# Modulation weights in column blocks: the opening of a hybrid decoder trunk on one core

## The chip, the cores and the metric

The kernel runs on one core of one Trainium2 chip. The metric is device time in microseconds (us). Inputs are float32.

## The reference, cut to what matters

One layer: a conditioning vector c gives shift and scale; the normed tokens are scaled and shifted; one wide projection feeds all branches. The part that the change touches is this.

```
mod = silu(c) @ w_ada + b_ada              # 1024 -> 3072
shift, mscale, gate = split(mod, 3)
h = rms_norm(x, norm_gain) * (1 + mscale) + shift     # (1024 tokens, 1024 features)
proj = h @ w_in                            # q, kv, gates, z_attn, u, z_ssm, merge gates
u = 256 columns of proj                    # input of the state-space branch
...                                        # attention, state space model, merge, final norm
```

Every feature of h needs its own shift and scale, and each of these is a sum over all 1024 entries of silu(c). A block of 128 features of h can be finished as soon as the 2 x 128 columns of w_ada that give its shift and scale are there. The products of u are sums over the 1024 features of h, so they can be accumulated block by block.

## The kernel before, in words

Five engines run queues of their own, in program order, tied by semaphores. What follows is the opening, up to the end of the products of u.

SyncE (SP) issues the large loads: eight tiles of x (L490), four row blocks of w_ada (L488; 128 rows by 2048 columns, 8 KB a row, 1 MB a block), the 256 columns of w_in that give u (L494, 1 MB), four more row blocks of w_ada, and then masks and tables. The next weights (`wraw`, L494) are loaded once the first have been split. GpSimd (POOL) issues 22 small loads for the state-space branch (L609 to L618) and then works through a chain of tiny operations (L601 to L650) that needs two Exp/Sin results of ScalarE.

ScalarE (ACT) takes Exp and Silu of small columns, then squares the eight x tiles as they come (`junk`), with a Sqrt after four and after eight. VectorE (DVE) scales the tiles to unit norm, four at a time (`xs`, L1158). TensorE (PE) transposes them in 16 groups of four (`xt`), evacuated in turn by ACT and DVE (L1163). Then PE sums the modulation: for each of eight row blocks, four matmuls with 32 columns of Silu(c) against 512 columns of w_ada (`ada_mm`), accumulated over all eight blocks into one bank. ACT copies the bank (`mrow`), PE transposes it, and DVE forms `modc` and `g1` for all features at once.

After that DVE, ACT and DVE work block by block (k = 0 to 7, 128 features each): xt times g1 plus modc (L1192), `ht_hi` as its rounded copy, `ht_lo` as the remainder (L1142). PE runs twelve matmuls for each k (four banks, three each: hi by hi, lo by hi, hi by lo) and accumulates u. On DVE the remainder of block k-1 stands behind the scaling of block k. Next on PE come the products of z_ssm (weights `whi[1]`, `wlo[1]`), then those of q. GpSimd waits for the last `ht_lo` and then prepares the state-space kernels, on which PE, ACT and SP rely later.

Of the kernel before, what the change touches and what calls it, by code (L numbers as in the profile page):

```python
# [22 lines left out]
P = 128  # L23
SEQ = 1024
D_MODEL = 1024
KT = D_MODEL // P
# [32 lines left out]
CW = 280  # L59
# [144 lines left out]
def build(nc, x, c, w_ada, b_ada, norm_gain, w_in, pe_cmp_k, w_cmp_k1, b_cmp_k1, w_cmp_k2,  # L204
# [6 lines left out]
    def at(name, shape, dt, offset):  # L211
        return nc.alloc_sbuf_tensor_at(name, shape, dt, offset=offset)
# [4 lines left out]

    ada = at("ada", [P, KT, 2048], F, R_H)
    ht_hi = at("ht_hi", [P, KT, SEQ], R, R_H)
# [28 lines left out]

    mrow = at("mrow", [P, HALF], F, R_W + KT * CW * 4 * 2)
    junk = at("junk", [P, D_MODEL], F, R_W + KT * CW * 4 * 4)  # L250
# [28 lines left out]
    scol = const("scol", [P, KT, 32], F)  # L279
    modc = const("modc", [P, 2 * KT], F)  # L280
    g1 = const("g1", [P, KT], F)
    ss = const("ss", [P, ST], F)
# [199 lines left out]
    with nc.Block() as block:  # L482
# [3 lines left out]
        def _(sp):  # L486
            def load_ada(k):
                sp.dma_start(ada[:, k, :], w_ada[0, P * k:P * k + P, 0:2048]).then_inc(s_blk[k], 16)  # L488
            def load_x(i):
# [107 lines left out]
        def _(pool):  # L597
# [213 lines left out]
        def _(act):  # L811
# [13 lines left out]

            act.wait_ge(once("pcol"), 1)
            a(dt_[:, :], pcol[:, 32:40], ACT.Exp).then_inc(once("dt"), 1)
            a(scol[:, :, :], pcol[:, 48:56].unsqueeze(2).to_broadcast([P, KT, 32]), ACT.Silu).then_inc(s_silu, 1)
            for i in range(ST):
                act.wait_ge(s_x[i], 16)  # L830
                if i >= 1:
                    act.wait_ge(s_sq, i)
                a(junk[:, :], xs[:, i, :], ACT.Square, accum_out=ss[:, i:i + 1]).then_inc(s_sq, 1)
                if i % 4 == 3:
                    act.wait_ge(s_var, i // 4 + 1)
                    a(rs[:, i - 3:i + 1], ss[:, i - 3:i + 1], ACT.Sqrt).then_inc(s_sd, 1)
            for cc in range(NC_HALF):
# [4 lines left out]
            act.wait_ge(once("pw_arg"), 1)  # L842

            a(pw[:, 1, :, :], pw[:, 1, :, :], ACT.Exp).then_inc(once("pw_fn"), 1)
            a(pw[:, 2, :, :], pw[:, 0, :, :], ACT.Sin, scale=SIN_2PI / 2).then_inc(once("pw_fn"), 1)
            a(pw[:, 3, :, :], pw[:, 0, :, :], ACT.Sin, scale=SIN_2PI).then_inc(once("pw_fn"), 1)

            def split_w(w):
# [5 lines left out]

            split_w(0)

            act.wait_ge(s_mod, 1)
            a(mrow[:, :], bank[0]).then_inc(once("mrow"), 1)


            for r in range(2):
                act.wait_ge(once("ctr"), 1)
                a(ct[r][:, :, :], bank[4][:, P * r:P * r + P].rearrange("p (t c) -> p t c", t=SSM_T))\
                    .then_inc(once("ctev"), 1)

            def fill(n):
                act.wait_ge(s_tr, n + 1)
                return bank[n % 2]

            for k in range(KT):  # L870
                for m, cols in enumerate(h_parts(k)):
                    act.wait_ge(s_h32, m + 1 if k == 0 else k + 2)
                    a(ht_hi[:, k, cols], xt[:, k, cols]).then_inc(s_hhi, 1)
            split_w(1)

# [241 lines left out]
            for k in range(KT):  # L1117
                act.wait_ge(s_blk[k], 32)
# [18 lines left out]
        def _(dve):  # L1137
# [26 lines left out]
            dve.wait_ge(s_id, 16)  # L1164
            V.tensor_copy(identb[:, :], ident[:, :]).then_inc(once("identb"), 1)
            dve.wait_ge(once("den"), 1)
            V.reciprocal(sm[:, 9, :], sm[:, 8, :]).then_inc(once("rden"), 1)
            dve.wait_ge(s_whi, 1)
            tt(wlo[0][:, :, 0:256], wraw[:, :, 0:256], f(whi[0][:, :, 0:256]), ALU.subtract).then_inc(s_wlo, 1)
            dve.wait_ge(once("pcol"), 1)  # L1170
            dve.wait_ge(once("mcol"), 1)
            mcol = bank[5].rearrange("p (q r) -> p r q", q=4)[:, ::32, :]
            ch.link(tt(modc[:, :].rearrange("p (b q) -> p b q", b=4), mcol,
                       bcol.rearrange("p (b q) -> p b q", b=4), ALU.add))
            ch.link(V.scalar_tensor_tensor(out=g1[:, :], in0=modc[:, KT:2 * KT], scalar=1.0, in1=gcol,
                                           op0=ALU.add, op1=ALU.mult))
            dve.wait_ge(once("xta"), 8)
# [18 lines left out]
            h_lo(KT - 1)  # L1196
            split_w(1)
            dve.wait_ge(s_small, 16 * 5)
# [385 lines left out]
        def _(pe):  # L1584
# [18 lines left out]

            def ada_mm(k):
                pe.wait_ge(s_blk[k], 16)
                for j in range(4):
                    ins = mm(bank[0][32 * j:32 * j + 32, :], scol[:, k, :], ada[:, k, j * HALF:(j + 1) * HALF],
                             k == 0, k == KT - 1)
                return ins
            pe.wait_ge(s_id, 16)  # L1610
# [3 lines left out]
            for n in range(16):  # L1614
# [10 lines left out]
                ins.then_inc(s_xtr, 1)  # L1625
            pe.wait_ge(s_silu, 1)
            for k in range(KT):
                ins = ada_mm(k)
            ins.then_inc(s_mod, 1)
            pe.wait_ge(once("cld"), 16 * 2 * SSM_T)  # L1630
            pe.wait_ge(once("xta"), 7)
            for r in range(2):
                ins = tr(bank[4][:, P * r:P * r + P], cld[r][:, :])
            ins.then_inc(once("ctr"), 1)
            pe.wait_ge(once("xtd"), 8)
            pe.wait_ge(once("mrow"), 1)
            for q in range(4):
                ins = tr(bank[5][:, P * q:P * q + P], mrow[:, P * q:P * q + P])
            ins.then_inc(once("mcol"), 1)


            def bank_free(n):
# [12 lines left out]


            pe.wait_ge(s_whi, 1)
            pe.wait_ge(s_wlo, 1)
            for k in range(KT):
                pe.wait_ge(s_hlo, 1 if k == 0 else k + 2)  # L1660
                for i in (0, 2, 1, 3):
                    ct_, cc = divmod(i, 2)
                    if k == 0 and i == 1:
                        pe.wait_ge(s_hlo, 2)
# [4 lines left out]
            ins.then_inc(s_unit, UU)  # L1669

            def project(w, tiles=range(ST)):
# [433 lines left out]
```

## Time and profile before

| | us |
|---|---|
| median of 3 runs | 992.6 (991.83 to 993.16) |
| the profiled execution, its own time | 991.09 |
| span in its trace | 989.3 |
| TensorE busy in the span | 910.2 (92%) |
| VectorE busy | 528.5 (53%) |
| ScalarE busy | 394.5 (40%) |
| GpSimd busy | 215.7 (22%) |

The span runs from the first to the last instruction; 1.8 us of the execution lie around it. TensorE's busy time overstates its work, since matmuls overlap. In the 40 slices of the profile TensorE is at nine tenths or more in nearly all slices; the two first slices (0 to 49 us) are the exception, with none and seven tenths, while the DMA engines are at nine tenths there.

### The profile page before, as it was taken

How to read it: one execution, taken by the hardware profiler on the slowest of the kernel's cores; microseconds unless marked ns; L12 is line 12 of the kernel's file. 1: busy time of each engine (PE TensorE's matmuls, PEld its weight loads, DVE VectorE, ACT ScalarE, POOL GpSimd, SP SyncE). 2: the span in 40 equal slices, each digit the busy share in tenths (PEclk: the TensorE clock that was granted, in tenths of full speed). 3: DMA queues.
4: the chain of work that ended last, by engine and by line, in shares of the span. 5: the costliest groups of instructions: out<-in, count | busy, mean ns of one | idle time of the engine just before them, and what ended most of it. 6: DMA issues, size and time to landing. Idle time of an engine off the chain costs nothing.

```text
span 989.3 us, 14340 instructions
## 1 busy us (share of the span) xinstructions
PE 910.2 (92%) x5573; PEld 745.6 (75%) x5581; DVE 528.5 (53%) x1075; ACT 394.5 (40%) x786; POOL 215.7 (22%) x213
## 2 busy tenths in 40 slices
PE   0799999899999999999998998889999999999996
PEld 0488999689999766666676766678888888877885
DVE  1561279426765487797786876552231222217543
ACT  5533232422123466767657667641111111114121
POOL 6249512111100112212203212145551000000000
PEclk9999999899999999999999999989999999999998
DMA  9917041031010000000000001043322112033222
GB/s 314 356 44 128 4 111 65 1 88 45 1 44 1 2 1 1 1 1 1 2 1 1 1 2 32 7 123 96 100 71 70 53 33 59 16 154 127 87 85 85
DMA packets 53716, 59.67 MB, mean 60 GB/s; under 512 B 10097, under 2 KB 45489, under 8 KB 52609
## 3 DMA queue, kind: packets, MB, share of 16 engines
q1 hardware_dynamic: 51392, 54.13, 18.3%
q0 software_dynamic: 2000, 4.54, 1.6%
q8 instruction: 44, 0.72, 0.3%
q14 instruction: 24, 0.19, 0.1%
q10 hardware_dynamic: 256, 0.09, 0.0%
HBM read 52.92 MB, written 5.24 MB: 59 GB/s over the span
## 4 chain that ended last, share of the span: by engine, by line
PE 71%; DVE 14%; ACT 6%; SPq 3%; issue 3%; DMA 2%; POOL 0%; DVEq 0%; ACTq 0%; POOLq 0%
PE bank L1588 39%; PE slc_max L1588 15%; PE win_max L1588 13%; PE bank L1591 3%; DVE plo L1142 3%; SPq L488 2%; DVE rt L1142 2%; DVE mx L1410 2%; DMA ada<-in_w_ada 2%; ACT pt L815 1%; DVE mx L1417 1%; ACT phi L815 1%; ACT osb L815 1%; DVE qa L1142 1%; SPq L527 1%
## 5 line engine op out<-in xcount | busy, mean ns | idle before, releaser
L1142 DVE TENSOR_TENSOR plo<-pt,phi 128x512 fp32r<-128x512 f32 x192 | 116.2, 621 | 36.8 <-ACT phi L815 36.4
L815 ACT ACTIVATE pt<-bank 128x512 f32<-128x512 f32 (+1 forms) x208 | 98.7, 474 | 83.3 <-PE bank L1588 77.2
L1588 PE MATMUL bank<-q,k 128*128 128x512 f32 (+7 forms) x384 | 102.7, 349 | 0.9
L815 ACT ACTIVATE phi<-bank 128x512 fp32r<-128x512 f32 (+1 forms) x208 | 98.5, 474 | 0.0
L601 POOL TENSOR_TENSOR qa<-qa,otmp 128x256 f32<-128x256 f32 x32 | 27.5, 859 | 215.2 <-DVE otmp L1142 215.2
L1588 PEld LDWEIGHTS bank<-q,k 128*128 128x128 f32 (+1 forms) x384 | 63.4, 190 | 11.9 <-ACT phi L815 2.9
L1588 PE MATMUL bank<-phi,vhi 128*65 128x512 f32 x192 | 70.1, 365 | 2.4 <-ACT osb L815 1.9
L1588 PE MATMUL bank<-phi,vlo 128*64 128x512 f32 x192 | 62.0, 323 | 0.0
L1588 PE MATMUL bank<-plo,vhi 128*65 128x512 f32 x192 | 61.9, 323 | 0.0
L1588 PE MATMUL bank<-ht_hi,dhi 128*128 128x512 f32 x128 | 50.6, 396 | 2.8 <-DVE at_lo L1142 2.8
L1410 DVE TENSOR_REDUCE mx<-slc_max 128x1 f32<-128x128 f32 (+3 forms) x64 | 48.1, 752 | 8.7 <-PE slc_max L1588 8.7
L815 ACT ACTIVATE dsig<-bank 128x512 f32<-128x512 f32 x16 | 9.6, 599 | 105.3 <-PE bank L1588 105.3
L1588 PE MATMUL win_max<-whi,ht_hi 128*128 128x256 f32 (+1 forms) x160 | 47.5, 297 | 4.2 <-ACT catc L815 4.2
L1588 PE MATMUL bank<-ht_lo,dhi 128*128 128x512 f32 x128 | 50.3, 393 | 0.0
L1588 PE MATMUL bank<-ht_hi,dlo 128*128 128x512 f32 x128 | 50.3, 393 | 0.0
L1588 PE MATMUL bank<-whi,ht_hi 128*128 128x256 f32 (+1 forms) x160 | 46.6, 291 | 0.0
L1588 PE MATMUL win_max<-wlo,ht_hi 128*128 128x256 f32 (+1 forms) x160 | 46.4, 290 | 0.0
L1588 PE MATMUL win_max<-whi,ht_lo 128*128 128x256 f32 (+1 forms) x160 | 46.3, 289 | 0.0
L1588 PE MATMUL bank<-wlo,ht_hi 128*128 128x256 f32 (+1 forms) x160 | 45.3, 283 | 0.0
L1588 PE MATMUL bank<-whi,ht_lo 128*128 128x256 f32 (+1 forms) x160 | 45.2, 283 | 0.0
L1417 DVE TENSOR_REDUCE mx<-win_max 128x1 f32<-128x640 f32 (+2 forms) x64 | 41.4, 648 | 0.0
L1142 DVE TENSOR_TENSOR mt<-bank,dsig 128x512 f32<-128x512 f32 x8 | 5.5, 692 | 63.3 <-ACT dsig L815 54.3
(395 smaller groups left out, 2535.8 us busy)
## 6 DMA issues: line engine op xcount, KB each, us to landing
ada<-in_w_ada SPq DMA_DIRECT2D x8, 1024.0 KB, 17.0
draw<-in_w_in SPq DMA_DIRECT2D x16, 512.0 KB, 3.9
wraw<-in_w_in SPq DMA_DIRECT2D x7, 1024.0 KB, 5.4
xs<-in_x SPq DMA_DIRECT2D x8, 512.0 KB, 10.9
gstage<-in_w_ada POOLq DMA_DIRECT2D x16, 256.0 KB, 3.1
oraw<-in_w_out SPq DMA_DIRECT2D x8, 512.0 KB, 6.5
xr<-in_x SPq DMA_DIRECT2D x8, 512.0 KB, 4.3
out<-yr SPq DMA_DIRECT2D x8, 512.0 KB, 2.9
```

Source lines behind the costliest of these rows:

```text
L488: sp.dma_start(ada[:, k, :], w_ada[0, P * k:P * k + P, 0:2048]).then_inc(s_blk[k], 16)
L527: sp.dma_start(toep[SC * i:SC * i + SC, :, SC * i:CH * SC], klag[:, :, 0:(CH - i) * SC])\
L601: return nc.gpsimd.tensor_tensor(o, a, b, op)
L815: return nc.scalar.activation(o, i, fn, **kw)
L1142: return V.tensor_tensor(o, a, b, op)
L1410: V.tensor_reduce(m[:, i, 1:2], slc_max[:, 0:P * (i + 1)], AX.X, ALU.max).then_inc(once("msr"), 1)
L1417: V.tensor_reduce(m[:, i, 2:3], win_max[:, 0:P * min(i + 1, WIN_TILES + 1)], AX.X, ALU.max)\
L1588: return T.matmul(o, l, r, start=start, stop=stop, **kw)
L1591: return T.transpose(o, i, ident[0:rows, 0:rows])
```

## The change: what it does

The weights of the modulation come in eight column blocks. Block j holds, for all 1024 rows, the 128 shift columns and the 128 scale columns of features 128j to 128j+127. It is 1 MB as before, loaded by four DMAs (two halves of the rows, shift and scale) in pieces of 512 bytes. The weights of u are loaded ahead of all of them, behind x.

On PE, `modulation_sums(k)` runs eight matmuls of 256 columns (two halves of four row blocks; the four blocks of a half stand in the four column groups of the array, so four partial sums come out), `modulation_columns(k)` two transposes. ACT copies the sums (`modulation_rows`), DVE adds the four parts and forms modc and g1 of this block (three small operations, then a wait). Two blocks are done ahead of the products of u. The sums of block k+2 stand on PE ahead of the products of block k, its transposes in the middle of them.

ScalarE's Exp and Silu move behind the fourth square, the split of u's weights between the two halves of the transposes, and the Exp and Sin of the state space (`state_functions`) into the block loop behind block 3. DVE splits the low part of u's weights in two halves inside the loop. GpSimd's small loads wait for the last tile of x.

```diff
-    ada = at("ada", [P, KT, 2048], F, R_H)
+    ada = at("ada", [P, 2, KT, 4, 2, P], F, R_H)
...
+            ada_view = w_ada[0, :, 0:2048].rearrange("(a q p) (m j f) -> a j m p q f", a=2, q=4, m=2, j=KT)
+            def load_ada(j):
+                for a_ in range(2):
+                    for m in range(2):
+                        sp.dma_start(ada[:, a_, j, :, m, :], ada_view[a_, j, m]).then_inc(s_blk[j], 16)
...
-            for k in range(4):
-                load_ada(k)
             load_w(0)
-            for k in range(4, KT):
-                load_ada(k)
+            for j in range(KT):
+                load_ada(j)
...
             pool.dma_start(ramp[:, :], t_ramp.to_broadcast([P, 160])).then_inc(s_ssmp, 16)
+            pool.wait_ge(s_x[ST - 1], 16)
...
+            def modulation_rows(k):                 # ScalarE
+                act.wait_ge(s_mod, k + 1)
+                if k >= 2:
+                    act.wait_ge(once("mcol"), k - 1)
+                a(mrow[k % 2][:, :, :], bank[4 + k % 2][:, 0:2 * P].rearrange("p (m f) -> p m f", m=2))\
+                    .then_inc(once("mrow"), 1)
...
+            modulation_rows(0)
+            modulation_rows(1)
             for k in range(KT):
                 for m, cols in enumerate(h_parts(k)):
                     act.wait_ge(s_h32, m + 1 if k == 0 else k + 2)
                     a(ht_hi[:, k, cols], xt[:, k, cols]).then_inc(s_hhi, 1)
+                if k + 2 < KT:
+                    modulation_rows(k + 2)
+                if k == 3:
+                    state_functions()
...
+            def modulation(k):                      # VectorE
+                dve.wait_ge(once("mcol"), k + 1)
...
+                ch.link(V.tensor_reduce(mpart[:, :], parts, AX.X, ALU.add))
+                ch.link(tt(mk, mpart[:, :], bcol..., ALU.add))
+                V.scalar_tensor_tensor(out=g1[:, k:k + 1], ...).then_inc(once("modc"), 1)
+                dve.wait_ge(once("modc"), k + 1)
...
             for k in range(KT):
+                modulation(k)
                 for cols in h_parts(k):
                     V.tensor_scalar(xt[:, k, cols], xt[:, k, cols], g1[:, k:k + 1], modc[:, k:k + 1], ALU.mult, ALU.add)
+                if k == 0:
+                    first_weights_low(0)
                 if k >= 1:
                     h_lo(k - 1)
+                if k == 1:
+                    first_weights_low(1)
...
+            for k in range(2):                      # TensorE
+                modulation_sums(k)
+                modulation_columns(k)
             pe.wait_ge(s_whi, 1)
+            pe.wait_ge(once("wlo0"), 1)
             for k in range(KT):
+                if k + 2 < KT:
+                    modulation_sums(k + 2)
...
                 pe.wait_ge(s_hlo, 1 if k == 0 else k + 2)
                 for i in (0, 2, 1, 3):
+                    if i == 1:
...
+                        if k + 2 < KT:
+                            modulation_columns(k + 2)
...
                     for m, (l, r) in enumerate(parts):
                         ins = mm(unit_bank(i), l[:, k, cs], r[:, k, ts], k == 0 and m == 0, k == KT - 1 and m == 2)
```

`modulation_sums(0)` waits until all of xt has been evacuated, since it uses the same banks.

## Rows read from the trace of the kernel before

**Rows 1.** The chain that ended last, 0 to 130 us: start, us, what.
```profile
25.82 17.13 DMA ada<-in_w_ada
...
48.48 1.41 PE bank L1588 x3
...
71.91 0.70 PE slc_max L1588 x3
```
**Rows 2.** The last x tile's DMA: duration ns, start, and its landing.
```profile
L490 SPq DMA_DIRECT2D xs<-in_x x1: 535/535/535, 4.3 to 4.3; - x1
DMA to landing us min/median/max: 14.0/14.0/14.0
```
**Rows 3.** Stretches: window, length, engines busy, PEclk, DMA share, GB/s.
```profile
5.00:11.00 6.00, 0.00 (x0) 0.00 (x0) 0.00 (x0) 0.30 (x1) 6.00 (x13) 1.00 1.05 234
11.00:18.00 7.00, 0.32 (x1) 0.18 (x1) 0.43 (x2) 5.71 (x10) 5.79 (x19) 1.00 1.04 365
18.00:27.00 9.00, 3.75 (x18) 3.76 (x19) 4.79 (x11) 7.95 (x15) 0.40 (x2) 1.00 1.01 421
760.00:762.00 2.00, 2.00 (x11) 1.65 (x10) 0.00 (x0) 0.00 (x0) 0.00 (x0) 1.00 1.11 317
```
**Rows 4.** The same view while ut, 16 partitions at a time, is loaded.
```profile
80.00:82.00 2.00, 2.00 (x11) 1.60 (x10) 0.00 (x0) 0.00 (x0) 2.00 (x1) 1.00 1.29 111
```
**Rows 5.** Timeline of the x stage: start, us, engine, line, what.
```profile
13.82 1.04 ACT L815 ACTIVATE junk<-xs 128x1024 f32<-128x1024 f32 x1
...
15.05 1.06 ACT L815 ACTIVATE junk<-xs 128x1024 f32<-128x1024 f32 x1
...
25.65 2.74 DVE L1158 TENSOR_SCALAR xs<-xs,rs 128x1024 f32<-128x1024 f32 x4
...
34.10 0.69 DVE L1163 COPY xt<-bank 128x512 f32<-128x512 f32 x1 [0.18 <-PE bank L1591]
```
**Rows 6.** Timeline from the modulation's sums to the first scaled block.
```profile
34.00 5.36 PE L1588 MATMUL bank<-ada,scol 128*32 128x512 f32 x48
...
44.12 0.60 ACT L815 ACTIVATE mrow<-bank 128x512 f32<-128x512 f32 x1 [4.76 <-PE bank L1588]
...
44.62 0.44 ACT L815 ACTIVATE ct<-win_max 128x128 f32<-128x128 f32 x2
...
44.86 0.63 PE L1591 MATMUL win_max<-ident,mrow 128*128 128x128 f32 x4 [0.44 <-ACT mrow L815]
45.60 0.17 DVE L1142 TENSOR_TENSOR modc<-win_max,pcol 128x16 f32<-128x16 f32 x1 [1.22 <-PE win_max L1591]
...
46.01 1.72 DVE L1192 TENSOR_SCALAR xt<-xt,g,modc 128x512 f32<-128x512 f32 x3
```
**Rows 7.** Timeline of the block loop: scaling, remainder, rounded copy.
```profile
52.57 0.81 DVE L1192 TENSOR_SCALAR xt<-xt,g,modc 128x1024 f32<-128x1024 f32 x1
53.30 1.22 DVE L1142 TENSOR_TENSOR ht_lo<-xt,ht_hi 128x1024 fp32r<-128x1024 f32 x1
...
57.13 1.06 ACT L815 ACTIVATE ht_hi<-xt 128x1024 fp32r<-128x1024 f32 x1 [0.80 <-DVE xt L1192]
```
**Rows 8.** TensorE in two stretches: busy, granted clock, DMA share, GB/s.
```profile
48.40:51.90 3.50, 3.42 (x9) 0.55 0.17 60
51.90:72.60 20.70, 20.70 (x90) 0.99 0.16 52
```
**Rows 9.** Timeline of ScalarE's state functions, first and last.
```profile
34.28 1.28 ACT L815 ACT_TABLE_LOAD   x1
...
37.15 0.42 ACT L815 ACTIVATE pw<-pw 128x72 f32<-128x72 f32 x2
```
**Rows 10.** Timeline of GpSimd after the last remainder.
```profile
61.80 0.40 POOL L601 TENSOR_TENSOR bbar<-sm,bb 128x128 f32<-128x128 f32 x1 [17.07 <-DVE ht_lo L1142]
...
107.92 2.40 POOL L601 TENSOR_TENSOR etmp<-etmp,etmp 128x1024 f32<-128x1024 f32 x1
118.94 1.81 POOL L714 MEMSET toep<- 128x2048 f32 x1 [8.63 <-PE bank L1591]
```

More of the change, by code:

```diff
@@ L247, in w_raw @@
         return z1raw if w == Z1_ else wraw
-    mrow = at("mrow", [P, HALF], F, R_W + KT * CW * 4 * 2)
+    mrow = [at(f"mrow{s}", [P, 2, P], F, R_W + KT * CW * 4 * 2 + 1024 * s) for s in range(2)]
     junk = at("junk", [P, D_MODEL], F, R_W + KT * CW * 4 * 4)
@@ L280, in build @@
     modc = const("modc", [P, 2 * KT], F)
+    mpart = const("mpart", [P, 2], F)
     g1 = const("g1", [P, KT], F)
@@ L824, in _ @@
             act.dma_start(prow[40:48, :], lam_im[0].rearrange("(t g) s -> t (g s)", g=2)).then_inc(s_prow, 16)
-            act.wait_ge(once("pcol"), 1)
-            a(dt_[:, :], pcol[:, 32:40], ACT.Exp).then_inc(once("dt"), 1)
-            a(scol[:, :, :], pcol[:, 48:56].unsqueeze(2).to_broadcast([P, KT, 32]), ACT.Silu).then_inc(s_silu, 1)
             for i in range(ST):
@@ L836, in _ @@
                     a(rs[:, i - 3:i + 1], ss[:, i - 3:i + 1], ACT.Sqrt).then_inc(s_sd, 1)
+                if i == 3:
+                    act.wait_ge(once("pcol"), 1)
+                    a(dt_[:, :], pcol[:, 32:40], ACT.Exp).then_inc(once("dt"), 1)
+                    a(scol[:, :, :], pcol[:, 48:56].unsqueeze(2).to_broadcast([P, KT, 32]), ACT.Silu).then_inc(s_silu, 1)
             for cc in range(NC_HALF):
@@ L841, in _ @@
                     a(xt[:, k, cc * HALF:(cc + 1) * HALF], bank[4 + n % 4]).then_inc(once("xta"), 1)
[L842 to L846, printed above, removed]
+                if cc == 0:
+                    act.wait_ge(s_raw, 16)
+                    a(whi[0][:, :, 0:256], wraw[:, :, 0:256]).then_inc(s_whi, 1)
             def split_w(w):
@@ L853, in split_w, with state_functions @@
                 a(w_parts(w)[0][:, :, 0:n], w_raw(w)[:, :, 0:n]).then_inc(s_whi, 1)
[L855 to L864, printed above, removed]
+            def modulation_rows(k):
[4 more added lines that the diff above has]
+                    .then_inc(once("mrow"), 1)
+            def state_functions():
+                act.wait_ge(once("pw_arg"), 1)
+                a(pw[:, 1, :, :], pw[:, 1, :, :], ACT.Exp).then_inc(once("pw_fn"), 1)
+                a(pw[:, 2, :, :], pw[:, 0, :, :], ACT.Sin, scale=SIN_2PI / 2).then_inc(once("pw_fn"), 1)
+                a(pw[:, 3, :, :], pw[:, 0, :, :], ACT.Sin, scale=SIN_2PI).then_inc(once("pw_fn"), 1)
             def fill(n):
@@ L873, in _ @@
                     a(ht_hi[:, k, cols], xt[:, k, cols]).then_inc(s_hhi, 1)
+                if k + 2 < KT:
+                    modulation_rows(k + 2)
+                if k == 3:
+                    state_functions()
+                if k == 5:
+                    for r in range(2):
+                        act.wait_ge(once("ctr"), 1)
+                        a(ct[r][:, :, :], bank[4][:, 256 + P * r:256 + P * r + P].rearrange("p (t c) -> p t c", t=SSM_T))\
+                            .then_inc(once("ctev"), 1)
             split_w(1)
@@ L1117, in _ @@
             for k in range(KT):
-                act.wait_ge(s_blk[k], 32)
+                act.wait_ge(s_blk[k], 80)
                 a(ohi[:, k, :], oraw[:, k, :]).then_inc(once("ohi"), 1)
@@ L1193, in _ @@
                         .then_inc(s_h32, 1)
+                if k == 0:
+                    first_weights_low(0)
                 if k >= 1:
                     h_lo(k - 1)
+                if k == 1:
+                    first_weights_low(1)
             h_lo(KT - 1)
+            dve.wait_ge(s_id, 16)
+            V.tensor_copy(identb[:, :], ident[:, :]).then_inc(once("identb"), 1)
+            dve.wait_ge(once("den"), 1)
+            V.reciprocal(sm[:, 9, :], sm[:, 8, :]).then_inc(once("rden"), 1)
             split_w(1)
@@ L1601, in three, with modulation_sums, modulation_columns @@
                 return ins
[L1604 to L1609, printed above, removed]
+            def modulation_sums(k):
+                pe.wait_ge(s_blk[k], 64)
+                if k == 0:
+                    pe.wait_ge(s_silu, 1)
+                    pe.wait_ge(once("xta"), 8)
+                    pe.wait_ge(once("xtd"), 8)
+                if k >= 2:
+                    pe.wait_ge(once("mrow"), k - 1)
+                o = bank[4 + k % 2]
+                for a_ in range(2):
+                    for q in range(4):
+                        ins = mm(o[32 * q:32 * q + 32, 0:2 * P], scol[:, 4 * a_ + q, :],
+                                 ada[:, a_, k, q, :, :].rearrange("p m f -> p (m f)"), a_ == 0, a_ == 1)
+                ins.then_inc(s_mod, 1)
+            def modulation_columns(k):
+                pe.wait_ge(once("mrow"), k + 1)
+                if k >= 2:
+                    pe.wait_ge(once("modc"), k - 1)
+                for m in range(2):
+                    ins = tr(bank[6 + k % 2][:, P * m:P * m + P], mrow[k % 2][:, m, :])
+                ins.then_inc(once("mcol"), 1)
             pe.wait_ge(s_id, 16)
@@ L1625, in _ @@
                 ins.then_inc(s_xtr, 1)
[L1626 to L1639, printed above, removed]
             def bank_free(n):
@@ L1662, in _ @@
                     ct_, cc = divmod(i, 2)
-                    if k == 0 and i == 1:
-                        pe.wait_ge(s_hlo, 2)
+                    if i == 1:
+                        if k == 0:
+                            pe.wait_ge(s_hlo, 2)
+                        if k + 2 < KT:
+                            modulation_columns(k + 2)
+                        if k == 3:
+                            pe.wait_ge(once("cld"), 16 * 2 * SSM_T)
+                            for r in range(2):
+                                ins = tr(bank[4][:, 256 + P * r:256 + P * r + P], cld[r][:, :])
+                            ins.then_inc(once("ctr"), 1)
                     cs, ts = slice(P * ct_, P * ct_ + P), slice(cc * HALF, (cc + 1) * HALF)
@@ L1669, in _ @@
             ins.then_inc(s_unit, UU)
+            pe.wait_ge(once("ctev"), 2)
             def project(w, tiles=range(ST)):
```

29 lines of the change are left out of this document (14 added, 15 removed).

## The prediction, made before the changed kernel was run

> **What bounds the kernel now.** I read the chain of waits first. Up to 42.95 us it is the load of w_ada; then sums, copies and the first scaled block lead to the first product of u at 48.48, and from there to 72.6 (71.91 and 0.70) it is PE [rows 1]. PE then goes straight on to z_ssm and stays the chain for tens of microseconds. So the change acts through one number, the time at which u's products end, now 72.6. I call it E and take what it moves as moving the whole run; the last part of this section's sum tests that. The view by stretches shows what the load costs: 234 GB/s while GpSimd's small loads run beside x, 365 behind them, 421 once w_ada's 8 KB rows run alone [rows 3]. The timeline shows the second line of work, which is hidden under the load now: the last xt is copied at 34.8 (34.10 and 0.69) [rows 5]. This is only 8 us before the load ends, and the change must put everything else behind it.
>
> **The load.** Same bytes. Pieces of 512 bytes of the same shape run in the late weight loads at 317 GB/s [rows 3]; the other row with 512-byte runs, into 16 partitions at a time, gives 111 [rows 4]. I take 317, since it fills 128 partitions as here, and keep 111 as the far end. x, freed of the small loads, should land by 14 (18.3 now: 4.3 and 14.0 [rows 2]; 4.2 MB at 365 from 2.5 on). u's weights follow by 17, then a block each 3.3 us (1.05 MB at 317), plus some 2.4 us for the small loads, which now run beside w_ada ((365 - 234) x 6 us at 317 [rows 3]). The last block lands at 17 + 26.5 + 2.4 = 46, 3 us later than now. SP issues 32 DMAs instead of 8 at about 0.5 us each; behind them wait the masks and the weights of z_ssm, both needed 20 us later.
>
> **The x stage.** ACT squares at the pace of 1.23 us (13.82 to 15.05) [rows 5] and can start when the first tile lands, near 5, not behind Silu. Four squares end at 10.2; a Sqrt with a table load of 1.28 [rows 9] ends at 11.7. Exp and Silu with two more table loads end at 15.2, the other four squares at 20.1, load and Sqrt at 21.7; DVE scales (2.74 [rows 5]) until 24.9. Now that ends at 28.4 (25.65 and 2.74), and the last copy of xt follows 6.4 us later [rows 5]. The split of u's weights on ACT, 1.9 us, comes in between and is not fully hidden: 1.2 us; if the transposes meet a slower PE, 1 us more. So xt is complete at 32.5 to 33.5, say 33.
>
> **From there to the first product.** Sums of a block: now eight instructions of 512 columns take 5.36 / 6 = 0.86 with the drain left out [rows 6]; sixteen of 256 columns are the same array time, 0.86. With drain and the copy to `mrow` (0.4, between 0.60 for 512 columns and 0.44 for two of 128 [rows 6]) and two transposes (0.4 of the 0.63 for four [rows 6]), DVE gets its columns 1.9 us after the start. Three small operations at 0.2 each (45.60 to 46.01 for two [rows 6]) make 0.6. Then DVE has in its queue: scaling of block 0 (0.9), half of the weights' low part (1.1; 1024 elements, as a remainder of 1.22 [rows 7]), modulation of block 1 (0.6), its scaling (0.7), half a remainder (0.6). Sum 1.9 + 0.2 + 0.6 + 0.9 + 1.1 + 0.6 + 0.7 + 0.6 + handoffs 0.3 = 6.9: the first product starts at 39.9, 8.6 us before now.
>
> **The block loop** decides. The products of block k+1 wait for its remainder; on DVE that stands behind the modulation and the scaling of block k+2, whose columns PE transposes only in the middle of the products of block k. So from one start of a block to the next: six matmuls 1.40 (two of the 0.70 steps [rows 1]), transposes 0.40, handoff 0.05, modulation 0.61, scaling 0.72 (52.57 to 53.30), remainder 1.22 [rows 7], handoff 0.14: 4.5 us. PE alone needs 2.8 + 0.86 + 0.24 = 3.9. Without the change it needs 2.8. Behind PE's wait stand the rest of the block and nothing else useful. The first block runs at the half clock: 1.41 for three matmuls, granted clock 0.55, then 0.99 [rows 1, 8]; PE is as sparsely busy before it as now. That makes the first step 6.0 (1.4 more, and slower transposes). At block 3 ACT stops for the state functions, 34.28 to 37.57 = 3.3 [rows 9], between `mrow` of block 5 and the rounded copy (1.06 [rows 7]) of block 4: sums of 5 end at 54.6, copy 55.0, functions 58.3, rounded copy 59.3, remainder and handoff 60.7. Starts of blocks 0 to 6: 39.9, 45.9, 50.4, 54.9, 60.7 (1.3 of it the stop), 65.2, 69.7. Blocks 6 and 7 have no sums left, so 2.8 each: E = 75.3, 2.7 us later than 72.6. The products leave the shadow of the last load, but each block pays 1.7 us more than now (4.5 for 2.8), and that over six blocks is more than the 8.6 us of head start.
>
> **What lies behind E.** The low part of z_ssm's weights now follows the last remainder (70.9) on DVE: two tiny operations 0.4, then 2.5: 73.8, 1.5 us before PE asks. GpSimd starts its state-space chain behind the last remainder. Now that is 61.8 and it ends at 110.3, with its next work released by PE at 118.9 [rows 10]: 8.6 us of slack. The last remainder comes 9.6 us later and E 2.7: a slack of 1.7 is left. Both cost nothing by a narrow margin; if they give, 0 to 2 us. GpSimd's own small loads end near 31 and its chain then waits for ScalarE in any case.
>
> The sum for the profiled execution is 991.1 + 2.7 = 993.8; the median of the runs shown is 1.5 above that execution, so 995.3.
>
> **Rivals.** (1) *PE paces the loop, not slower than before.* If DVE's small operations overlap more, the step is PE's 3.9; with xt at 32 and no half clock, starts run 38.9 + 6 x 3.9, the stop costs 1.9, E = 38.9 + 23.4 + 1.9 + 5.6 = 69.8, minus 2.8: 989.8. It decides if the handoff path is under 3.9. For it: DVE's operations overlap by 0.1 each (52.57 + 0.81 is after 53.30 [rows 7]). Against: every term of the path has its row, and they add to 4.5.
> (2) *The load paces, as the description has it.* Sums of block 7 follow its landing at 46, E = 46 + 1.1 + 4.5 + 5.6 = 57.2, so 977. It would need block 5 to start at 47; but blocks 0 to 5 have landed before half of the loop is run, and xt is not there before 32. In this forecast only the first two blocks' products run beside a load at all.
> (3) *The clock stays low.* If the gaps in the loop (0.6 of 4.5) keep the granted level at 0.55, that is 1.2 GHz, a block costs 5.1 + 1.7 + 0.5 = 7.3 us: E = 39.9 + 43.8 + 10.2 = 93.9, so 1014. In the trace the level rises within a gapless stretch [rows 8]; no row shows a loop with short gaps, but PE would be busy for 3.9 of 4.5 us, so 0.05. The Trainium skill (TensorE: Matmul & The Clock Gate, "HAM oscillation") says that a matmul loop that waits between its tiles can fall back to half clock in every tile, which here is this rival.
> (4) *512-byte pieces at 111 GB/s* [rows 4]: a block lands each 9.4 us, the last at 95, E = 106, so 1026.
>
> **Chances.** Forecast 0.60, (1) 0.25, (2) 0.07, (3) 0.05, (4) 0.03. The forecast's own range is 992 to 999 (xt at 32 to 36, step 4.2 to 5.0, margins behind E giving up to 2). The range over the cases is 988 to 1001: it leaves out (2), (3), (4) and the edges. A measurement of this kernel tells no change from about 2 us (0.2%). Slower by more: 0.42 of the forecast, (3) and (4): 0.50. Within: 0.16 of the forecast and 0.12 of (1): 0.28. Faster: 0.02, 0.13 of (1), (2): 0.22.
>
> **What would show it.** In the timeline after: the last copy of xt near 33; the first product of u near 40, at 0.43 a matmul; then starts of blocks 4.5 apart, with PE idle 0.6 before each, released by DVE's `ht_lo`; one step near 5.8 behind Exp and Sin; the last w_ada landing near 46, long before its sums run. I am wrong if PE waits for a DMA in the loop, if its idle time there is nil, if the loop's granted clock is near 0.5, or if the state-space part waits for GpSimd's chain.

## The result, and the profile after

| | before | after |
|---|---|---|
| median of 5 runs each, side by side, us | 992.66 (991.83 to 993.16) | 996.6 (996.33 to 997.18) |
| ratio | | 1.0040 (0.95 interval 1.0026 to 1.0055) |
| the profiled execution, its own time | 991.09 | 996.41 |
| span in its trace | 989.3 | 994.6 |
| E, the end of u's products | 72.6 | 76.6 |

Slower by 0.4%; the forecast was 995.3. The time before lies 1.6 us over its profiled execution, the time after 0.2, so the medians are 3.9 us apart and the spans 5.3. Most of the 1.6 belongs to the kernel before itself. In the 58 further executions of it that ran beside the experiments, 22 had a granted clock of 0.987 to 0.989 over the whole execution and a median of 990.9, and 36 had 0.984 to 0.986 and a median of 992.5; the profiled one (991.09, at 0.987) is of the first kind.

The page of the kernel after, its first two parts (busy time, then 40 slices of 24.9 us). TensorE stands at one tenth in the first slice (before: none), at seven in the second as before, and the load (DMA at nine tenths) still fills both:

```profile
span 994.6 us, 14580 instructions
PE 914.9 (92%) x5657; PEld 748.3 (75%) x5657; DVE 533.2 (54%) x1098; ACT 399.2 (40%) x795; POOL 215.7 (22%) x213
PE   1789999799999999998998998889999999999996
PEclk9899999999999999999999999989999999999998
DMA  9938042032010000000000001043322112033222
```

The chain of waits of the kernel after, 0 to 90 us (start, us, what), which answers to [rows 1]. Before, its first long piece is the DMA of w_ada up to 42.95 and its second PE. Now no DMA stands in it after 9.1 us; it goes through ScalarE's squares, VectorE's scaling and the transposes, and then once round four engines in each block:

```profile
1.62 7.49 DMA xs<-in_x
...
22.81 2.74 DVE xs L1175 x4
...
34.08 1.10 PE win_max L1622 x16
35.20 0.39 ACT mrow L819
...
46.81 0.97 PE bank L1622 x3
47.78 0.70 PE slc_max L1622 x3
48.48 0.23 PE bank L1625 x2
48.73 0.18 DVE mpart L1196
48.93 0.18 DVE modc L1159
49.13 0.17 DVE g L1198
49.36 0.69 issue
50.05 1.23 DVE ht_lo L1159
51.33 0.97 PE bank L1622 x3
...
54.61 1.04 PE win_max L1622 x16
55.67 0.38 ACT mrow L819
56.08 1.28 ACT L819
...
57.65 1.28 ACT L819
58.94 0.42 ACT pw L819 x2
59.36 0.96 ACT ht_hi L819
60.34 1.26 DVE ht_lo L1159
61.74 0.93 PE bank L1622 x3
...
76.59 11.17 PE win_max L1622 x48
```

From 46.81 to 51.33 one round can be read off: six matmuls, two transposes, VectorE's three small operations, the scaling (the 0.69 that the chain writes as "issue"; VectorE's timeline has the scaling at 49.33, 0.81 long), the remainder, PE. That is 4.52 us, against the 2.8 of twelve gapless matmuls. From 54.61 on, the same round is held up by the state functions: two table loads of 1.28 and two times `pw`.

The stretches of the kernel after (window, length, then the engines' busy time from PE to POOL, PEclk, DMA share, GB/s), which answer to [rows 3, 8]. The first is the one with GpSimd's small loads, the second w_ada alone; the last two are PE's first block and the rest of the loop:

```profile
20.00:26.00 6.00, 0.81 (x4) 0.42 (x4) 3.54 (x7) 4.11 (x7) 6.00 (x11) 0.79 1.25 213
34.00:50.00 16.00, 12.85 (x96) 7.93 (x96) 9.77 (x22) 4.47 (x8) 0.00 (x0) 0.89 1.21 290
41.00:46.00 5.00, 5.00 (x26) 3.61 (x30) 3.28 (x7) 0.51 (x1) 0.00 (x0) 0.70 1.22 292
46.00:76.00 30.00, 26.40 (x171) 18.00 (x164) 18.05 (x33) 13.10 (x19) 8.14 (x18) 1.00 0.42 114
```

GpSimd of the kernel after, timeline (start, us, engine, line, what), which answers to [rows 10]: the idle time before the last of these, in which it waits for PE, is its slack: 0.60 where it was 8.63.

```profile
72.22 2.61 POOL L604 TENSOR_TENSOR sm<-sm 128x8 f32<-128x8 f32 x2 [7.14 <-DVE sm L1230]
74.91 0.67 POOL L604 TENSOR_TENSOR bbar<-sm,bb 128x128 f32<-128x128 f32 x1
...
119.98 2.35 POOL L604 TENSOR_TENSOR etmp<-etmp,etmp 128x1024 f32<-128x1024 f32 x1
122.93 1.81 POOL L718 MEMSET toep<- 128x2048 f32 x1 [0.60 <-PE bank L1625]
```

### The profile page after: what moved, and what is told of

It reads as the page before. It is cut to its first block, busy times and chain, and to the rows that moved or that the text cites. A ratio compares the mean times of both kernels' runs of the same rounds, so it can differ in the third digit from the quotient of the medians.

```text
span 994.6 us, 14580 instructions
## 1 busy us (share of the span) xinstructions
PE 914.9 (92%) x5657; PEld 748.3 (75%) x5657; DVE 533.2 (54%) x1098; ACT 399.2 (40%) x795; POOL 215.7 (22%) x213
## 4 chain that ended last, share of the span: by engine, by line
PE 72%; DVE 16%; ACT 8%; issue 3%; DMA 1%; SPq 0%; POOL 0%; DVEq 0%; ACTq 0%
PE bank L1622 39%; PE slc_max L1622 15%; PE win_max L1622 13%; PE bank L1625 4%; DVE plo L1159 3%; DVE rt L1159 2%; DVE mx L1444 2%; DVE mx L1451 1%; ACT pt L819 1%; ACT phi L819 1%; ACT osb L819 1%; ACT L819 1%; DVE qa L1159 1%; DMA xs<-in_x 1%; ACT junk L819 1%
```

## The experiments

The theory is the forecast's: the round through ACT, PE and VectorE paces the loop at 4.5 us, and E carries into the whole. The rivals left are the load, and PE's own work. Each run is read at two places: E, and its median beside runs of the kernel before on the same chip (992.13 to 992.44 in two of the three groups, 991.58 in the first).

### The load: half the bytes

```diff
                 for a_ in range(2):
                     for m in range(2):
-                        sp.dma_start(ada[:, a_, j, :, m, :], ada_view[a_, j, m]).then_inc(s_blk[j], 16)
+                for m in range(2):
+                    sp.dma_start(ada[:, 0, j, :, m, :], ada_view[0, j, m]).then_inc(s_blk[j], 32)
...
-                                 ada[:, a_, k, q, :, :].rearrange("p m f -> p (m f)"), a_ == 0, a_ == 1)
+                                 ada[:, 0, k, q, :, :].rearrange("p m f -> p (m f)"), a_ == 0, a_ == 1)
```

This leaves out the lower half of w_ada's rows; the sums take the upper half twice.

> The changed kernel with half of the modulation weights: only the first 512 rows are loaded (two DMAs a block, half the bytes) and used for both halves of the sums, so that TensorE's work is the same and the modulation differs. Theory (the loop runs behind the landings): the last block lands near 36 for 51, but the step stays 4.5 and E between 75.6 and 76.6, time 995.6 to 996.6. Rival (the load sets the loop, or slows the engines beside it): E at least 4 us earlier, 992.6 or less.

Measured: 997.15 (995.01 to 999.96), ratio 1.0059 (1.0037 to 1.0082): no gain over the kernel after. TensorE's timeline in this run, the first matmul of blocks 1 and 2 with the idle time before it, shows the old step of 4.5:

```profile
45.22 0.50 PE L1621 MATMUL bank<-ht_hi,whi 128*128 128x512 f32 x1 [0.24 <-DVE ht_lo L1158]
49.74 0.50 PE L1621 MATMUL bank<-ht_hi,whi 128*128 128x512 f32 x1 [0.24 <-DVE ht_lo L1158]
```

E is 75.0, just under the 75.6 to 76.6 expected. That is 1.6 before the kernel after, but not by the load: in this trace the first block's products ran at the full clock (1.00 in 41 to 46 us, where the kernel after shows 0.70), and the kernel after has E = 75.1 in a second execution with the full clock there (see "The kernel after once more"). The load has no part in E; the rival in which it paces is out.

### The round: transposes later

The two transposes of the next columns stand behind the ninth matmul of a block and not behind the sixth. Nothing is added.

```diff
                     for i in (0, 2, 1, 3):
                         if i == 1:
...
-                            if k + 2 < KT:
-                                modulation_columns(k + 2)
...
+                        if i == 3 and k + 2 < KT:
+                            modulation_columns(k + 2)
```

> The changed kernel with one edit: the transposes of the next modulation columns stand behind nine of a block's twelve products, not behind six. E is the time at which u's products end (76.6 us in the changed kernel, 72.6 before). Theory (the handoff path sets the loop's step: six products, transposes, modulation, scaling, remainder = 4.5 us): three products more in the path, 0.70 us per step, in six steps, less the slack at the state functions: E near 80.5, time near 1000.5. Rival (TensorE's own 3.9 us plus something fixed per block sets the step): E unchanged, 996.6. Rival (the load sets it): unchanged.

Measured: 1001.6 (999.05 to 1002.26), ratio 1.0097 (1.0080 to 1.0115). The same rows of TensorE's timeline:

```profile
46.16 0.50 PE L1622 MATMUL bank<-ht_hi,whi 128*128 128x512 f32 x1 [0.93 <-DVE ht_lo L1159]
51.38 0.50 PE L1622 MATMUL bank<-ht_hi,whi 128*128 128x512 f32 x1 [0.93 <-DVE ht_lo L1159]
```

The step is 5.2: three matmuls of 0.23 were put into the round and each block got 0.7 longer, with the idle time up from 0.24 to 0.93. Were PE's own work the pace, the move would have cost nothing. E is 80.1. At the loop's end the granted clock fell too; the view by stretches has the last of it:

```profile
74.00:76.00 2.00, 2.00 (x6) 1.55 (x5) 1.67 (x2) 0.40 (x1) 1.74 (x2) 0.50 0.01 4
```

0.50 is the 1.2 GHz level. It came behind the longest gap of this loop (1.94 us, before block 6), and eight matmuls took some 0.43 and not 0.23 each, 1.5 us in all. The first block ran at the full clock here, which gained about as much. So it is by two effects that cancel that E came out near the expected 80.5; the step of 5.2 depends on neither.

### The round: remainder first, and the state functions earlier

```diff
             for k in range(KT):
+                if k >= 1:
+                    h_lo(k - 1)
                 modulation(k)
                 for cols in h_parts(k):
                     V.tensor_scalar(xt[:, k, cols], ...)
                 if k == 0:
                     first_weights_low(0)
-                if k >= 1:
-                    h_lo(k - 1)
```

```diff
                     a(ht_hi[:, k, cols], xt[:, k, cols]).then_inc(s_hhi, 1)
+                if k == 1:
+                    state_functions()
                 if k + 2 < KT:
                     modulation_rows(k + 2)
-                if k == 3:
-                    state_functions()
```

The first alone, the second alone, then both:

> The changed kernel with one edit: on VectorE the remainder of block k-1 stands ahead of the modulation and scaling of block k, so that a block's products no longer wait for the next block's modulation. Theory: the first product comes 1.3 us earlier (39.6 for 40.9), the step falls from 4.5 to TensorE's 3.9, the stop at block 3 grows from 1.3 to 2.0 us; E near 72.3 for 76.6, time near 992.3. Rival (the load of 512-byte pieces or the clock sets the step): E falls by at most the 1.3 of the start, 995.3 or more. Rival (GpSimd's chain, which starts behind the last remainder and has 0.6 us of slack): E falls but the time stays within 1 us of 996.6.

> The changed kernel with one edit: ScalarE's Exp and Sin of the state space stand behind the rounded copy of block 1, where ScalarE is idle for 5.1 us, instead of behind the sums' copy of block 5. Theory: the stop of 1.3 to 1.4 us between the products of blocks 3 and 4 goes, E near 75.2, time near 995.2; the chain on GpSimd does not start earlier, since it waits for the last remainder. Rival (the step into block 4 is long for another reason): E unchanged, 996.6.

> The changed kernel with both edits together: the remainder ahead of the modulation on VectorE, the state functions behind block 1 on ScalarE. Theory (handoff path and stop are the two losses of the loop): the stop of 1.9 us that the first edit still had goes, E near 71.8 for 73.65; the last remainder is then 3.1 us ahead of E, so that GpSimd's chain (49.9 us from the last remainder to its end, wanted 46.3 behind E) comes 0.5 us late; time near 992.1. Rival (the time no longer follows E, since GpSimd's chain is the bound): 993.0 or more.

| | E | median | ratio (interval) |
|---|---|---|---|
| remainder first | 73.7 | 993.95 | 1.0031 (1.0014 to 1.0048) |
| functions earlier | 73.7 | 994.73 | 1.0039 (1.0024 to 1.0053) |
| both | 71.8 | 993.14 | 1.0011 (1.0002 to 1.0019) |

With the remainder first, PE starts blocks 0 to 3 without any idle time. TensorE's timeline of that run; the sums of block 4 and, with no idle time named, the first matmul of block 2 (that of block 1 starts at 45.03):

```profile
48.24 1.07 PE L1622 MATMUL win_max<-ada,scol 128*32 128x256 f32 x16
49.24 0.50 PE L1622 MATMUL bank<-ht_hi,whi 128*128 128x512 f32 x1
```

The step is 4.2 and PE is the pace: twelve matmuls 2.79, transposes 0.22, sums 1.00, and 0.2 more for the first three matmuls behind the sums (0.90 and not 0.70). So 0.3 us a block was the order of two operations on VectorE. The stop behind block 3 stays (1.7 idle; 2.0 was expected). E was 73.7 and not the 72.3 expected: the step is 4.2 and not the expected 3.9, and the x stage ended 0.8 later in this trace; the full clock in the first block (1.00 in 41 to 46 us) took back about 1.5. With the functions earlier alone the step into block 4 falls from 5.9 to 4.6 and the rest stays at 4.5; E was 1.5 below the expected 75.2 because the first block had the full clock in this execution (1.00 in 41 to 46 us, see below). The medians tell less: 1.0039 for the earlier functions can't be told from the 1.0040 and 1.0057 of the kernel after; it is E, 73.7 against 75.1 with the same full clock, that shows the gain. Both give E = 71.8, as expected, and it is below the 72.6 of the kernel before.

The time of both together is nevertheless over that of the kernel before: 993.14 against 992.44, where 992.1 was expected and 993.0 or more was the rival's figure (GpSimd's chain is the bound). Two views of that run say where it went. First GpSimd's chain, with no idle time left before its last step:

```profile
116.43 2.38 POOL L604 TENSOR_TENSOR etmp<-etmp,etmp 128x1024 f32<-128x1024 f32 x1
118.88 1.81 POOL L718 MEMSET toep<- 128x2048 f32 x1
```

In the chain of waits of that run, what follows is no longer PE's: GpSimd's last operation, seven DMA issues and their landing, a copy on ScalarE, and VectorE's start on the state-space scan (`b_r`):

```profile
121.45 0.74 POOL klag L604
...
128.78 2.73 DMA toep<-klag
...
132.08 0.60 ACT b_i L819
...
132.75 0.07 DVE b_r L1275
```

The kernel before has the same rows with `klag` at 121.52 and `b_r` at 132.66: the 0.8 us won at E are gone there. Second a stretch in the attention, 610 to 615 us, where the kernel before shows a granted clock of 1.00. First the row of both edits, then that of before:

```profile
610.00:615.00 5.00, 4.61 (x15) 3.15 (x16) 1.50 (x7) 1.71 (x7) 0.73 (x1) 0.52 0.00 0
```

```profile
610.00:615.00 5.00, 4.55 (x28) 3.46 (x29) 2.42 (x10) 3.12 (x9) 0.73 (x1) 1.00 0.00 0
```

At the half clock PE got 15 matmuls through in the time of 28. This is discussed below.

### The side edits

Two runs ask what the edits around the blocks are worth. One puts GpSimd's small loads back beside x; the other takes the kernel before and gives it only the earlier x stage: the small loads behind x, Exp and Silu behind the fourth square, u's weights ahead of w_ada.

```diff
-            pool.wait_ge(s_x[ST - 1], 16)
```

```diff
+            pool.wait_ge(s_x[ST - 1], 16)
             for gp in range(2):
...
-            for k in range(4):
-                load_ada(k)
             load_w(0)
-            for k in range(4, KT):
+            for k in range(KT):
                 load_ada(k)
...
-            a(dt_[:, :], pcol[:, 32:40], ACT.Exp).then_inc(once("dt"), 1)
-            a(scol[:, :, :], ..., ACT.Silu).then_inc(s_silu, 1)
             for i in range(ST):
...
+                if i == 3:
+                    a(dt_[:, :], pcol[:, 32:40], ACT.Exp).then_inc(once("dt"), 1)
+                    a(scol[:, :, :], ..., ACT.Silu).then_inc(s_silu, 1)
```

> The changed kernel without the wait of GpSimd's small loads. Theory: they run beside x as before, the fourth tile lands near 12.5 for 9 and the last near 18 for 15.6; xt is complete 2 us later, near 36, since now the x stage leads to the first product; E near 78.6 and time near 998.6. Rival (the x stage has slack to the first product): E unchanged, 996.6.

> The kernel before with only the opening's side edits: u's weights loaded ahead of the modulation's, Exp and Silu behind the fourth square, GpSimd's small loads behind the last x tile; row blocks, sums and loop as before. Theory: xt is complete 2 to 3 us earlier but the load of w_ada, with the same rate of 421 GB/s, still ends near 43 and sets E: E 72.6 plus or minus 0.5 and time within 1 us of before. Rival (the earlier x stage itself is worth something): E 1 us or more earlier.

Small loads at once: 998.37, ratio 1.0067 (1.0053 to 1.0081), E = 78.1, near the expected 998.6 and 78.6. VectorE's and ScalarE's timeline, the fourth square and the last copy of xt. The square waited for its tile; in the kernel after it starts at 10.37, and the last copy is over at 33.9:

```profile
13.32 1.06 ACT L818 ACTIVATE junk<-xs 128x1024 f32<-128x1024 f32 x1 [1.37 <-DMA xs<-in_x]
...
36.10 0.69 DVE L1179 COPY xt<-bank 128x512 f32<-128x512 f32 x1 [0.18 <-PE bank L1624]
```

So the wait for the last x tile is worth 2.9 us at the first sums and 3.0 at E (78.1 against 75.1, both with the full clock in the first block). Of the median it is worth 1.3 to 2.0 us: this run lies 5.9 over the kernel before, the kernel after 3.9 and 4.6. The earlier x stage alone: 993.05, ratio 1.0011 (1.0002 to 1.0020); xt is complete at 33.6 and not 34.8 (2 to 3 us were expected), and the chain is, as before, the load of w_ada up to 42.9. E is 73.8, later than the 72.1 to 73.1 expected: the first product came 1.2 later (49.65), since the sums' tail and the transposes of the modulation fell into a slower clock (granted 0.71 in 41 to 46, where before has 1.00; the four transposes take 1.10 and not 0.63 [rows 6]).

So an earlier x stage gained nothing while the load was last, and once it was not, every microsecond of it was in E.

### Pushing on

Three more kernels carry both edits of the loop and, on top, the sums of a block one block earlier (those of block 3 ahead of block 0) and two transposes for GpSimd moved from block 3 to block 5 (ScalarE's copy of them from block 5 to block 6). They differ in GpSimd's start: the first lets its chain begin behind the remainder of block 5 and puts VectorE's reciprocal for it inside the loop; the second (below: final) has that reciprocal too, but lets GpSimd wait for the last remainder, as the kernel after does; the third (final2) has VectorE do the modulation ahead of the remainder and the scaling behind it.

```diff
                 modulation_columns(k)
+            for k in range(2, 4):
+                modulation_sums(k)
...
-                if k + 2 < KT:
-                    modulation_sums(k + 2)
+                if k >= 1 and k + 3 < KT:
+                    modulation_sums(k + 3)
...
-                        if k == 3:
+                        if k == 5:
...
+                if k == 6:
+                    dve.wait_ge(s_id, 16)
+                    V.tensor_copy(identb[:, :], ident[:, :]).then_inc(once("identb"), 1)
+                    dve.wait_ge(once("den"), 1)
+                    V.reciprocal(sm[:, 9, :], sm[:, 8, :]).then_inc(once("rden"), 1)
```

and in the first of the three alone:

```diff
-            pool.wait_ge(s_hlo, NH)
+            pool.wait_ge(s_hlo, 7)
```

and in the third alone:

```diff
-                if k >= 1:
-                    h_lo(k - 1)
                 if k == 6:
...
                 modulation(k)
+                if k >= 1:
+                    h_lo(k - 1)
                 for cols in h_parts(k):
```

> As the kernel with both edits, and three more: the sums run one block further ahead (those of block 3 fall into TensorE's wait before the first product), GpSimd's chain starts after the remainder of block 5 instead of the last, with VectorE's reciprocal for it inside the loop, and the transposes of c stand in block 5. Theory: one block's sums (1.0 us) leave the loop, E near 70.8, GpSimd is early again, time near 990.6, faster than before by 1 to 2 us. Rival (GpSimd's work beside VectorE slows the loop): E no earlier than 71.8.

> As the kernel with both edits, with the sums one block further ahead, and GpSimd's chain again behind the last remainder; only VectorE's reciprocal for it stands inside the loop, so that GpSimd's two small products are done before. Theory (VectorE was slowed by GpSimd beside it, and that took the gain of the last version): remainders take 1.22 us again, E near 70.9, GpSimd's chain 1 us early, time 1.5 us under that of before in the same comparison. Rival (the sums ahead bring nothing, since VectorE's and ScalarE's handoffs pace the loop at 3.7 and more): E 71.6 or later, time not under that of before.

> As the last one, with the order on VectorE modulation of block k, remainder of block k-1, scaling of block k: the three small operations fill the 1.1 us in which VectorE waits for the rounded copy. Theory: if VectorE and ScalarE pace the loop, E comes up to 1 us earlier than in the last one; if TensorE does, E is the same within 0.3.

| | E | median | ratio (interval) |
|---|---|---|---|
| GpSimd from block 5 on | 71.6 | 993.55 | 1.0015 (1.0005 to 1.0025) |
| final | 70.2 | 990.59 | 0.9988 (0.9979 to 0.9997) |
| final2 | 71.0 | 992.07 | 1.0006 (0.9997 to 1.0015) |

Why the early start lost is in its timeline, VectorE and GpSimd side by side:

```profile
65.42 1.95 POOL L604 TENSOR_TENSOR gs<-pw,bbar 128x1024 f32<-128x1024 f32 x1
66.15 2.30 DVE L1159 TENSOR_TENSOR ht_lo<-xt,ht_hi 128x1024 fp32r<-128x1024 f32 x1 [1.13 <-ACT ht_hi L819]
67.45 2.81 POOL L604 TENSOR_TENSOR b_r<-pw,bbar 128x1024 f32<-128x1024 f32 x1
68.37 4.03 DVE L1159 TENSOR_TENSOR wlo<-wraw,whi 128x2048 fp32r<-128x2048 f32 x1
...
72.55 0.47 PE L1623 MATMUL win_max<-ht_hi,whi 128*128 128x512 f32 x1 [0.98 <-DVE wlo L1159]
```

The remainder takes 2.30 us where it takes 1.22 elsewhere [rows 7], the weights' low part 4.03 and not 2.29, and PE waits 0.98 for it. So E is 71.6, but the products of z_ssm start at 72.55, where the kernel before starts them at 72.61: the gain is gone. Each ends as if VectorE had stood still until GpSimd's running operation was over: 65.42 + 1.95 + 1.22 = 68.6 (measured 68.45), 67.45 + 2.81 + 2.29 = 72.55 (measured 72.40). The Trainium skill (SBUF — State Buffer, "Who interferes with whom") has this rule: a VectorE instruction with two SBUF inputs and a GpSimd one that reads SBUF exclude each other, and the first to start keeps the interface for its whole length. These rows agree.

The second leaves GpSimd out of the loop, and its remainder is back at 1.23. It is the one kernel here that beats the kernel before, by 0.12%, on an interval that barely leaves out 1: E is 2.4 us earlier and the median 1.5, less than the 2 us that the forecast took as the least that a measurement tells. GpSimd bounds it: its chain, which starts behind the last remainder, has no idle time left before the `toep` step (one operation ends at 116.99, the next starts at 117.05), so the scan moves by 1.9 and not by 2.4. The last order of VectorE was no better than the remainder first: E is 0.8 later.

### The kernel after once more

> The changed kernel as it is, for comparison in the same call. Theory: starts of the blocks' products 4.5 apart again; E 76.6 if its first block runs at half clock, 75.2 to 75.4 if at full clock; time 995.3 to 996.6.

Measured: 996.74 (995.85 to 999.8) beside 992.13, ratio 1.0057 (1.0040 to 1.0074). The median repeats, but E in its trace is 75.1 and not 76.6. The first block in its timeline (and so in the runs with half the load, the later transposes, and the earlier functions) ran at the full clock; the stretch of 41 to 46 us:

```profile
41.00:46.00 5.00, 4.76 (x33) 3.16 (x33) 3.92 (x7) 1.24 (x3) 0.00 (x0) 1.00 1.18 289
```

Same kernel, 1.00 in one execution and 0.70 in the other, 1.5 us apart. Of the eleven traces of the kernel after and of the kernels made from it, only the first one shows less than 1.00 in this stretch.

## Why the prediction was right

The time was forecast 1.3 us too low (995.3 for 996.6), and E as well (75.3 for 76.6). That the two errors are equal is luck. The profiled execution was forecast at 993.8 and took 996.41, 2.6 more: 1.3 of it came in up to E, 1.3 behind E. The forecast then added 1.5 for the median over the profiled execution, which the kernel after doesn't show (0.2). The 1.5 came from the kernel before, whose profiled execution was one of its shorter ones. The mechanism is the forecast's; of the other ways, (2) and (4) fall with the load, (3) with the clock, and (1), PE as the pace, is what the loop becomes when the remainder goes first.

**The load.** The direction and the irrelevance were right, the sizes off. 512-byte pieces moved at 290 GB/s, not 317, at a DMA share of 1.21 where whole rows show 1.01 [rows 3]; 213 beside GpSimd's small loads; the last block landed at 51.1 and not 46. The Trainium skill (DMA: Bandwidth & Descriptors, "Specifications") puts the line rate at transfers of 512 bytes and more; at exactly 512 this trace has 0.69 of the 421 that 8 KB rows reach. SP was 39.95 us at the 32 issues and not some 16 (0.73 to 6.95 us each, from 5.2 to 45.1); what was queued behind them was not missed. Half the bytes changed nothing.

**The x stage.** xt complete at 33.9 against 33. The third tile landed at 9.1, so the fourth square ended 1.3 later than forecast (11.5 for 10.2); the rest of the stage kept its lengths, and a little was made good. This 0.9 is in every later start.

**From there to the first product.** From the start of the sums it took 6.84 us, from the last xt 6.98; 6.9 was forecast.

**The loop.** Its steps came out as 5.9 (first block, half clock), 4.5, 4.5, 5.9 (the stop), 4.5, 4.5, against the forecast's 6.0, 4.5, 4.5, 5.8, 4.5, 4.5. The measured starts, 40.92 to 70.73, are each 0.9 to 1.0 later than forecast, which is the x stage. Blocks 6 and 7 took 5.86 for 5.6: E = 76.6 for 75.3. The total of a step was right by terms that cancel. Its six matmuls took 1.67 and not 1.40 (0.97 and 0.70; the first three behind a wait are longer), the transposes 0.23 and not 0.40, and the last handoff 0.05 and not 0.14. The idle time before each start is 0.24 and not 0.6, because PE's own work in a step is near 4.2 and not 3.9: the sums take 1.00 without a wait behind them and not 0.86, and the matmuls behind them 0.2 more than counted. As the round sets the step, this cost nothing, and it shrank the gain that an ideal overlap would have had (4.2 and not 3.9 a block). The runs with later transposes (+0.7 for 0.7) and with the remainder first (4.2, no idle time) show the round as the cause; that was argued before and is shown now.

**The half clock of the first block** was right for the profiled execution by luck. The repeated run had the full clock there, as had all the other kernels made from this one. Without it the forecast of E would have been 73.9, for the 75.1 measured in the repeated run.

**The clock in the loop.** 1.00 from 46 us on, at gaps of 0.24 in 4.5 us and two of 1.40 and 1.24, so rival (3) is out. The rule named there (TensorE: Matmul & The Clock Gate, "HAM oscillation", in the Trainium skill) is not refuted by that, since its example waits longer than it works; the run with gaps of 0.93 in 5.2 and one of 1.94 did lose the clock, once.

**What lies behind E.** The low part of z_ssm's weights was ready at 74.8, 1.8 before PE asked (forecast 1.5). GpSimd's slack was 0.6, forecast 1.7. The last remainder ended 10.6 later than before (71.90 for 61.31) and not 9.6, which is the x stage again. GpSimd's chain began 13.1 later: it waited for VectorE's reciprocal at 71.95, which now stands behind the last remainder, and then two small operations beside the split of the weights took 2.61 us where 0.50 is their time in the run called final. What followed was 1.1 shorter, so the chain ended 12.0 later. That was still enough, but only just, and it became the chain as soon as E was moved forward.

**E carries into the whole.** Shown as far as the state-space scan, and only in part beyond it. Four places of the traces against those of the kernel before, in us (E; VectorE's start on the scan; the load of `draw`, near 603; ScalarE's first `dsig`, near 654), and the span:

| | E | scan | draw | dsig | span |
|---|---|---|---|---|---|
| before | 72.6 | 132.7 | 603.4 | 653.6 | 989.3 |
| after | +4.0 | +4.4 | +4.5 | +4.9 | +5.3 |
| after, once more | +2.5 | +2.7 | +4.1 | +4.4 | +4.7 |
| both edits | -0.8 | +0.1 | +0.2 | +3.9 | +4.3 |
| final | -2.4 | -1.9 | -1.7 | -1.5 | -1.4 |

In after, once more, and both edits, 1 to 4 us come in behind E that no edit explains. In both edits they lie at 605 to 660 us, where PE has gaps in every kernel and the clock falls for a while: before, in 640 to 650 only (0.76, 0.55 by stretches of 5 us); both edits and final2 in 610 to 615 as well (0.52, 0.50). That the clock differs there is shown. For both edits and final2 the other executions show that it is not the rule: the profiled one was the slowest of eleven in each (995.41 and 994.62), with a clock of 0.982 over the whole execution. One other in each had 0.982 (994.91 and 994.34); the remaining nine had 0.984 to 0.989 and took at most 993.67 and 993.27. So the 4.3 of the span is not what both edits cost; by the medians it is 0.7. Why the clock falls there in some executions is open. None of the 58 executions of the kernel before had 0.982, so the kernel may still have a part in it. Nor do these stretches explain the 1.4 us that the repeated run adds between the scan and `draw`. So the 2.7 of the forecast, the 2.5 to 4.0 at E and the 3.9 to 4.6 of the medians agree in sign and size, and the kernel before's profiled execution, 1.6 under its median, lengthens every difference of spans; but the way from E to the median is followed in one trace per kernel only, and 1 to 2 us of the medians have no place.

## What to carry to other kernels

Before a load is cut up so that its consumer can run beside it, write down the smallest round: what one block passes through, engine by engine, with what stands ahead of it on each in-order queue, and compare that with the consumer's gapless time. Here it was 4.5 against 2.8 for six blocks, 10.2 us and a stop of 1.4 on top, more than the 7.6 us (48.48 to 40.92) by which the first product came earlier; an order in which the urgent small operation goes first, and the long functions where their engine is idle, brought it to PE's own 4.2, and the run called final to a gain of 0.12%. An engine off the path that reads the same memory can nearly double the very operation everyone waits for (2.30 for 1.22). And before a profiled execution is compared with another, see where each lies among the times of its own kernel: here one was 1.6 under its median, another 2.3 over.

## What the runs showed of the hardware that was not expected

- 512-byte pieces: 290 GB/s at a DMA share of 1.21; 8 KB rows 421 at 1.01 [rows 3].
- One kernel, two executions: granted clock 0.70 and 1.00 in the same 5 us behind the sums.
- One kernel (before), 58 executions: a median of 990.9 where the clock over the execution was 0.987 to 0.989, of 992.5 where it was 0.984 to 0.986.
- VectorE's two-input operations beside GpSimd's: 2.30 for 1.22 and 4.03 for 2.29; the other way, GpSimd's small ones 2.61 for 0.50.
- SP's issue of a DMA took 0.73 us at best and up to 6.95 while 32 of them queued.
